# Gate table of a PEER layer: one-hot rows and gates in bf16, with each float32 gate in three pieces

## The reference, cut to what matters

```python
top, pos = lax.top_k(cand, PK_TOPK)
eidx = jnp.take_along_axis(cidx, pos, axis=-1)
gate = jax.nn.softmax(top, axis=-1)
act = jax.nn.gelu(jnp.einsum('thkd,td->thk', u_tab[eidx], xb), approximate=False)
return jnp.einsum('thk,thkd->td', gate * act, v_tab[eidx])
```

## Time and profile before

| | us |
|---|---|
| median of 3 runs | 2311.88 (2308.03 to 2314.87) |
| the profiled execution, its own time | 2312.38 |
| its span, first to last instruction | 2310.3 |
| PE busy | 2190.7 |
| DVE busy | 1722.2 |
| ACT busy | 923.1 |
| POOL busy | 902.6 |

### The profile page before, as it was taken

How to read it: one execution, slowest core, us unless ns; L and a number is a source line. 1 busy time by engine, 2 the same in 40 slices (tenths; PEclk the granted TensorE clock), 3 DMA queues, 4 the chain that set the end, 5 groups by cost and what they waited for, 6 DMA issues and landing times.

```text
span 2310.3 us, 40012 instructions
## 1 busy us (share of the span) xinstructions
PE 2190.7 (95%) x15622; PEld 2016.3 (87%) x15622; DVE 1722.2 (75%) x3100; ACT 923.1 (40%) x1585; POOL 902.6 (39%) x1063
## 2 busy tenths in 40 slices
PE   6999997998899999999999999999999999999997
PEld 4666886985589999888999999999999999999996
DVE  4657576545755555578899898888867799899888
ACT  3333342221232222221445688777733333333332
POOL 4321310111225555256221054344443466467652
PEclk9988998999979999999999999999999999999999
DMA  5542740225749999588776399999999999999994
GB/s 170 165 138 92 239 131 16 72 61 159 254 131 296 286 295 292 157 263 277 216 239 221 125 386 374 339 379 357 367 387 398 376 400 402 385 405 383 394 394 165
DMA packets 306619, 611.55 MB, mean 265 GB/s; under 512 B 29344, under 2 KB 194224, under 8 KB 305408
## 3 DMA queue, kind: packets, MB, share of 16 engines
q0 software_dynamic: 89968, 315.00, 38.1%
q1 hardware_dynamic: 198032, 268.83, 34.1%
q10 hardware_dynamic: 18432, 25.17, 2.9%
HBM read 484.45 MB, written 124.45 MB: 264 GB/s over the span
## 4 chain that ended last, share of the span: by engine, by line
PE 62%; DVE 22%; DMA 10%; issue 3%; ACT 2%; POOL 1%; SPq 0%; DVEq 0%; ACTq 0%; POOLq 0%
PE PS L1288 62%; DMA RAW<-in_vT 6%; DVE LO L2670 4%; DVE ACC L2870 3%; DVE arena L2011 2%; DMA u_rows<-CBLK 1%; DVE WL L2704 1%; DMA RAW<-in_uT 1%; DVE AIN L2699 1%; POOL u_rows L654 1%; ACT HI L1151 1%; DVE GU L2850 1%; DMA u_rows<-arena 1%; DMA u_rows<-TQ 1%; DMA GQ<-gate_table 1%
## 5 line engine op out<-in xcount | busy, mean ns | idle before, releaser
L1151 ACT ACTIVATE HI<-RAW 128x1024 fp32r<-128x1024 f32 x256 | 271.3, 1060 | 394.5 <-PE PS L1288 207.9
L2670 DVE TENSOR_TENSOR LO<-RAW,HI 128x1024 fp32r<-128x1024 f32 x256 | 312.4, 1222 | 125.4 <-ACT HI L1151 104.9
L798 POOL DMA_INDIRECT GU<-u_rows,EIDX x160 | 232.9, 1456 | 390.1 <-DVE ACTG L2850 286.9
L1288 PE MATMUL PS<-HT,W 128*128 128x272 f32 (+1 forms) x1504 | 357.3, 397 | 11.4 <-DVE HT L2058 11.4
L806 POOL DMA_INDIRECT GROW<-in_vT,EIDX x160 | 290.7, 1817 | 193.9 <-DVE ACC L2870 134.2
L1288 PE MATMUL PS<-XH,HI 128*128 128x384 f32 x1024 | 350.6, 342 | 13.8 <-DVE LO L2670 12.4
L1288 PE MATMUL PS<-WH,HI 128*128 128x384 f32 x1024 | 344.5, 336 | 7.5 <-DVE WL L2704 4.1
L1288 PEld LDWEIGHTS PS<-HT,W 128*128 128x128 f32 (+1 forms) x1504 | 282.3, 189 | 78.5 <-issue 19.0
L1288 PE MATMUL PS<-WL,HI 128*128 128x384 f32 x1024 | 343.3, 335 | 0.0
L1288 PE MATMUL PS<-WH,LO 128*128 128x384 f32 x1024 | 343.2, 335 | 0.0
L1288 PE MATMUL PS<-XL,HI 128*128 128x384 f32 x1024 | 343.1, 335 | 0.0
(11 more groups left out here) (292 smaller groups left out, 3681.9 us busy)
## 6 DMA issues: line engine op xcount, KB each, us to landing
RAW<-in_uT SPq DMA_DIRECT2D x128, 512.0 KB
RAW<-in_vT SPq DMA_DIRECT2D x128, 512.0 KB
arena<-in_uT POOLq DMA_DIRECT2D x78, 512.0 KB, 5.2
W<-in_w_in SPq DMA_DIRECT2D x58, 512.0 KB, 6.6
u_rows<-arena POOLq DMA_DIRECT2D x216, 128.0 KB, 3.9
table_a<-AX ACTq DMA_DIRECT2D x128, 192.0 KB
gate_table<-GST SPq DMA_DIRECT2D x48, 512.0 KB
AIN<-table_a SPq DMA_DIRECT2D x128, 192.0 KB
```

The source lines that it names most:

```text
L798: pool.indirect_dma_start(out=GU[n % NGU][0:P], out_offset=None, in_=flat_u, in_offset=bass.IndirectOffsetOnAxis(ap=at, axis=0)).then_inc( ...
L1151: nc.scalar.activation(HI[:, s % NRING], RAW[:, s % NRING], ACT.Copy).then_inc(S("hi"), 1)
L1288: return nc.tensor.matmul(out, lhsT, rhs, start=first, stop=last)
L2670: dve.tensor_tensor(LO_[:, s % NRING], RAW[:, s % NRING], HI[:, s % NRING].bitcast(F32), ALU.subtract).then_inc(S("lo"), 1)
```

## The change

Keys and one-hots become bf16. Each float32 gate is split by `pick_rows` into three bf16 pieces (rounded gate, rounded rest, rounded rest of that), kept in GT3. On DVE `one_hots` makes the comparison in bf16 and, behind a wait for its own semaphore `oheq`, a second instruction multiplies the row key's one-hots by the three pieces: 3 x 4 x 128 = 1536 columns; both instructions read one operand with a step of zero in the innermost dimension (`bc(..., 3, P)`). The ACT step `gated_hots` is gone. PE makes three bf16 products for each token, added in PSUM, twelve for a unit in place of four float32 ones. OH has four buffers in place of five; `units_slot` and `copy_slot` (and with it the stores of the gates) come one slot earlier.

```diff
--- before.py
+++ after.py
@@ -66,7 +66,7 @@
 EQT = 8
 GPARTS = 4
 NQT = NK // EQT
-NOH = 5
+NOH = 4
 NRING = 3
 NAX = 4
 NGR = 7
@@ -232,19 +232,14 @@
     return 36 + u * 76 // (8 * NEB)
 
 
-def gated_slot(u):
-
-    return hots_slot(u) + 1
-
-
 def units_slot(u):
 
+    return hots_slot(u) + 2
+
+
+def copy_slot(u):
+
     return hots_slot(u) + 3
-
-
-def copy_slot(u):
-
-    return hots_slot(u) + 4
 
 
 def units_at(slot_of, s):
@@ -354,18 +349,21 @@
 
 
         AX = sb("AX", [P, NAX, ND])
-        IT = sb("IT", [P, 3, ND])
+        IT = sb("IT", [P, 2, ND], BF16)
+        GT3 = sb("GT3", [P, 3, ND], BF16)
+        REST = sb("REST", [P, P])
+        IOTB = sb("IOTB", [P, P], BF16)
         GATX, ACTX, WGTX, SELX = [sb(n, [P, NX]) for n in ("GATX", "ACTX", "WGTX", "SELX")]
         EIDX2 = sb("EIDX2", [P, 2, NX], U32)
         WGT, GATG, ACTG = [sb(n, [P, P]) for n in ("WGT", "GATG", "ACTG")]
         EIDX = sb("EIDX", [P, 2, P], U32)
         GU = [sb(f"GU{i}", [P, D]) for i in range(2)]
-        spare = NCBLK + DT * T - NAX * ND - 3 * ND - 6 * NX - 5 * P - 2 * D
+        spare = NCBLK + DT * T - NAX * ND - 5 * ND // 2 - 3 * P // 2 - 6 * NX - 5 * P - 2 * D
         assert spare >= 0
         sb("spare", [P, spare])
         HI, LO_ = [sb(n, [P, NRING, DT * P], F32R) for n in ("HI", "LO")]
         XH, XL = [sb(n, [P, DT, ND], F32R, part) for n in ("XH", "XL")]
-        OH = sb("OH", [P, NOH, 2, 4, P], stack=part)
+        OH = sb("OH", [P, NOH, 5, 4, P], BF16, part)
         part.close()
         sb("XHL", [P, 2 * DT * ND], stack=part)
         TQ = sb("TQ", [P, 4, D], stack=part)
@@ -375,7 +373,7 @@
         part.close()
         YO = sb("YO", [P, DT, T], stack=part)
         part.close()
-        sb("XHLOH", [P, 2 * DT * ND + NOH * 8 * P])
+        sb("XHLOH", [P, 2 * DT * ND + NOH * 10 * P])
         RAW = sb("RAW", [P, NRING, DT * P])
         XTOK, XTOKX = [sb(n, [P, D]) for n in ("XTOK", "XTOKX")]
         GU += [sb(f"GU{i}", [P, D]) for i in range(2, NGU)]
@@ -1220,14 +1218,6 @@
                 act.wait_ge(S("dot"), DOT_AT["x", NX - 1] + 1)
                 nc.scalar.activation(ACTX[:], ACTX[:], ACT.Gelu).then_inc(S("dactx"), 1)
 
-            def gated_hots(u):
-
-                act.wait_ge(S("oheq"), u + 1)
-                for x in range(4):
-                    hot = OH[:, u % NOH, 1, x]
-                    ins = nc.scalar.activation(hot, hot, ACT.Copy, scale=IT[:, 2, 4 * u + x:4 * u + x + 1])
-                ins.then_inc(S("oh1"), 1)
-
             def copy_unit(u):
 
                 k = u // 8
@@ -1254,8 +1244,6 @@
                             spread_ranks(t, i)
                     if s == exp_slot(t):
                         exp_gates(t)
-                for u in units_at(gated_slot, s):
-                    gated_hots(u)
                 for u in units_at(copy_slot, s):
                     copy_unit(u)
                 for g in range(P // EB):
@@ -1981,8 +1969,10 @@
                     slot_free(pe, 2)
                 else:
                     pe.wait_ge(S("ge"), u - 2)
+                hots = OH[:, u % NOH]
                 for x in range(4):
-                    ins = mul(gate_bank(u)[:, x * P:(x + 1) * P], OH[:, u % NOH, 0, x], OH[:, u % NOH, 1, x])
+                    for i in range(3):
+                        ins = mul(gate_bank(u)[:, x * P:(x + 1) * P], hots[:, 0, x], hots[:, 2 + i, x], i == 0, i == 2)
                 ins.then_inc(S("ohf"), 1)
 
             pe.wait_ge(S("xsplit"), 1)
@@ -2823,7 +2813,15 @@
 
                 c0, m = PTILES[t]
                 dve.wait_ge(S("rows"), t)
-                copy(IT[:, :, c0:c0 + m], PS[:, t % 2, 1, 0:3 * P].rearrange("p (a b) -> p a b", a=3))
+                picked_, gate = PS[:, t % 2, 1, 0:2 * P], PS[:, t % 2, 1, 2 * P:3 * P]
+                if t == 1:
+                    copy(IOTB[:], iota[:])
+                copy(IT[:, :, c0:c0 + m], picked_.rearrange("p (a b) -> p a b", a=2))
+                for i in range(3):
+                    piece = GT3[:, i, c0:c0 + m]
+                    copy(piece, REST[:] if i else gate)
+                    if i < 2:
+                        tt(REST[:], REST[:] if i else gate, piece, ALU.subtract)
 
             def top_part(t, part):
 
@@ -2834,8 +2832,12 @@
 
                 if u >= NOH:
                     dve.wait_ge(S("ohf"), u + 1 - NOH)
-                dve.tensor_tensor(OH[:, u % NOH], bc(bc(iota[:], 1, 4), 1, 2), bc(IT[:, 0:2, 4 * u:4 * u + 4], 3, P),
+                hots, cols = OH[:, u % NOH], slice(4 * u, 4 * u + 4)
+                dve.tensor_tensor(hots[:, 0:2], bc(bc(IOTB[:], 1, 4), 1, 2), bc(IT[:, :, cols], 3, P),
                                   ALU.is_equal).then_inc(S("oheq"), 1)
+                dve.wait_ge(S("oheq"), u + 1)
+                dve.tensor_tensor(hots[:, 2:5], bc(hots[:, 1], 1, 3), bc(GT3[:, :, cols], 3, P),
+                                  ALU.mult).then_inc(S("oh1"), 1)
 
             def dot(n):
```

## The result

The changed kernel takes 2434.91 us (median of 4 runs, 2432.79 to 2437.30) against 2312.05 us before: a ratio of 1.0509, with a 95% interval of 1.0488 to 1.0530. The forecast was 2433 us.

A forecast was written before the change was run, and what follows sets the result against it. PE was taken to bound the gate units, with DVE becoming the bound after the change: 2312.4 + 105.7 + 18.4 + 1.8 + 3 − 8 = 2433 us. The range was 2400 to 2480 us, held 8 times in 10.

The forecast's parts named there:

- 0.52 us of slack a unit: PE-bound gate units, 1331.5 to 1667.7 us: 43.5 us DVE idle over 83 units; DVE bounds above about 1.65 us.
- The term that decided: DVE's comparison and product in the gate units: 1.04 ns a column, a unit 2.91 us in place of 1.13, +1.78.
- the double-rate rival: DVE's gate units: bf16 alone gives double rate, a unit 1.57 us, time 2305 to 2320, likeliest 2309 us; chance 0.10.
- The argument from broken runs: DVE's new operations: zero step resembles short-run or strided bf16 rows (about 1 and 2.1 ns a column), not fast 0.52 ns.
- The sum: Whole kernel: 2312.4 + 105.7 + 18.4 + 1.8 + 3 − 8 = 2433 us.
- 3 for idle time: Gate units on DVE: DVE idles a little even where it is the bound, +3 us, own range 0 to 15.
- The tail: DMA-bound part from slot 112 on: some six 0.5 MB transfers fewer outstanding, −8 us, between 0 and −15.
- where I had +1.8: DVE before the gate units: one pick_rows at +1.5 us plus 0.3 us for the copy of iota.
- twelve bf16 products at 0.8 us: PE's gate unit: twelve 128-column products take 0.8 us, near column rate, against 0.81 for float32; 1.57 at worst.
- a granted clock under 0.95 in the stage: Gate units on PE: a clock under 0.95 in the stretch was named as showing the prediction wrong.
- the clock rival: Gate units on PE: waiting lowers PE's clock, +30 to +70 us, 2460 to 2500 us; chance 0.11.
- The fourth buffer: One-hot buffers in the gate units: four in place of five is free, since PE finishes its units in time.

The follow-up runs named there:

- The first run: Changed kernel with comparison and product both reading a packed row of 128 elements in place of one element 128 times: 2309.58 us, ratio 0.9986.
- the later run with repeated runs of four: Changed kernel with one-hots laid out four tokens innermost, one unit at a time, PE reading at a step of four elements: 2375.13 us, ratio 1.0249.
- the short product: Changed kernel with only the product reading a packed row, the comparison left as it was: 2355.48 us, ratio 1.0179.
- The run at 16 bytes: Changed kernel with one-hots laid out eight tokens innermost, DVE operations for two units, PE reading at a step of eight elements: 2538.08 us, ratio 1.0957.

## Why the prediction was right, point by point

**The bound and the threshold.** That PE bounds the stage with 0.52 us of slack a unit on DVE was right: 0.45 us more cost 5 us, 0.99 us more cost 41 us, and at 1.57 us a unit both engines are full.

**The rate of the two operations.** The term that decided was taken from the rows whose operands don't run along neighbours. It was forecast at 1.22 and 1.75 us and measured at 1.219 and 1.758; a unit at 2.91 and measured at 2.93. The first run shows the cause: a packed row in the operand's place gives 0.68 and 0.96 us, as the double-rate rival priced them, and 2309.6 us, where that rival stood at 2309. The Trainium skill, "Vector Engine (DVE) Microarchitecture Reference", section 5.1, states the single rate for one element read 16 times; the trace agrees, for 128 times (1219 against 683 ns). The Trainium skill, "VectorE: DVE Perf Modes", section "Rules for kernel authors", gives bf16 tensor_tensor the double rate for dense, step-1 data; the run with packed rows agrees. A repeated element is not such data.

The argument from broken runs was weaker than it reads. Next to the two slow rows of line 2011 in the earlier trace rows the same trace has one that the prediction left out, 1024 columns in runs of four:

```profile
L2011 DVE TENSOR_TENSOR arena<-arena 128x1024 bf16<-128x1024 bf16 x4 | 3.0, 742 | 0.1
```

That is (742 − 160)/1024 = 0.57 ns a column, near the double rate, as the later run with repeated runs of four confirms. A broken run as such doesn't lose the rate; runs of two, single elements (in a row that writes float32) and the repeated element did. What carried the choice was that no fast row had a zero step.

**The sum.** The forecast put 127 us on the units (105.7, 18.4 and 3 for idle time) and +121.5 were measured. Of DVE's 4.9 us of idle time in the stretch 3.3 us are the gaps before the product (by the page), which already stand in the 2.91 us, so 1.6 are left where I had +3. The tail gave back 4.6 us where I had −8; in two runs built on the kernel before (four buffers, 256 columns more) it took 68.9 and 70.0 us in place of 71.5, so even of the 4.6 a part may be scatter, and no run isolates the transfers that I gave as the reason. The 7.6 us ahead of the first slot were not forecast and have nothing to do with the change. Without them the profiled executions would differ by 117 us where the terms add up to 121. So small misses on both sides cancel, and that the forecast lies 2 us from the median is luck.

**pick_rows.** The first one, with the copy of iota, starts and ends with these lines:

```profile
1264.46 0.22 DVE L2016 CAST IOTB<-iota 128x128 bf16<-128x128 f32 x1
...
1266.41 0.23 DVE L2016 CAST GT<-REST 128x128 bf16<-128x128 f32 x1
```

1264.46 to 1266.64 us, 2.2 us in place of 0.56: +1.6, where I had +1.8. The stretch that holds it came out 0.2 us shorter all the same; over the other runs it scatters by about 4 us (166.5 to 170.6).

**PE.** I priced twelve bf16 products at 0.8 us; at 0.056 us each they hold PE for 0.68 us. It made no difference. The prediction named a granted clock under 0.95 in the stretch as a sign that it was wrong. That sign came, 0.93, and the time was right all the same: the sign was badly chosen, since a lower clock costs nothing while PE waits for DVE. So the clock rival's premise came true and its +30 to +70 us did not: with eight of twelve products gone the clock fell further and the time stayed, and with the short product it rose to 0.99 and only DVE's 77 us came back. ACT, forecast at about a third busy in the stretch, was busy for 40% of it (210.1 of 520.9 us), of no effect either.

**Buffers and slots.** The fourth buffer is free, as forecast: in the changed kernel DVE waits for nothing, and in the PE-bound kernel before, with four buffers, it waits for PE at no cost in time, a case that the forecast did not cover. For the earlier slots no run stands by itself; the sum leaves no room for a large effect.

## What to carry to other kernels

Before work moves from one engine to another, divide the receiving engine's idle time in that stage by the number of steps: here 0.52 us a unit, and +1.80 was put on it. A narrower type buys DVE's double rate only if every operand runs along neighbours in its innermost dimension (runs of four were enough here, runs of two were not the earlier trace rows); an element repeated by a zero step costs about 1.04 ns a column in bf16 as in float32. A layout that mends that for one engine has to be priced on the engine that reads it.

## What I had not expected of the hardware

- PE's products slow down with the step of their operands: 0.056, 0.117 and 0.234 us for 128 columns of bf16 at steps of 2, 8 and 16 bytes. Both operands had the step, so which of them costs is open. The Trainium skill, "Advanced Engine Details and Errata", section "Memory Cachelines", speaks of 16-byte lines in SBUF, full speed from two accesses to a line on, and a penalty where each access meets another line. The run at 16 bytes agrees; at 8 bytes, with two elements in a line, the time has already doubled, so the measurement differs from it there.
- Small DVE operations with two per-partition scalars last 0.31 us for 128 columns, with one scalar 0.25 us, and came every 0.21 us on the mean.
- An fp32r product of 128 columns does not run at the column rate of the one with 384: four last 0.56 us, (0.56 − 0.27)/3 = 0.10 us each where 0.06 was expected.
